# Moving a Fourier mixer into the attention steps of a two-block transformer kernel, with a half-spectrum transform

## The reference, cut to what matters

```
h = x
mod = silu(c) @ w_mod[0] + b_mod[0]          # sh1, sc1, g1, sh2, sc2, g2
u = modulate(rms_norm(x, norm1_g), sh1, sc1)
f, q, k, v = split(u @ w_in_even)            # f: 512 wide, 4 groups of 128
y_four = Re(FFT over tokens and the 128 features of a group of f)  @ w_four[group]
y_att  = window_attention(q, k, v, context keys and values, rpb)
h = h + g1 * (concat(y_four, y_att) @ w_out_even)
...
```

## Time and profile before

| what | value |
|---|---|
| median of 3 runs | 1970.37 us (1966.52 to 1971.26) |
| the profiled execution | 1971.28 us, of which the span is 1969.5 us |
| PE busy | 1932.1 us, 98% |
| DVE, ACT, POOL busy | 967.1, 685.3, 944.7 us |
| mean granted TensorE clock | 0.993 |

### The profile page before, as it was taken

One profiled execution on the slowest core, in us unless ns is written; L12 is line 12 of the kernel. 1 busy time (PEld: TensorE's weight loads), 2 busy tenths in 40 slices (PEclk: granted clock), 3 DMA queues, 4 the chain that ended last, 5 costly groups with the idle time before them and its releaser, 6 DMA issues. The chain is left out here.

```text
span 1969.5 us, 25202 instructions
## 1 busy us (share of the span) xinstructions
PE 1932.1 (98%) x9932; PEld 1587.5 (81%) x9932; DVE 967.1 (49%) x1515; ACT 685.3 (35%) x907; POOL 944.7 (48%) x699
## 2 busy tenths in 40 slices
PE   7998999999999999999999999999999999999998
PEld 6875787888888888888888667888888888888886
DVE  4666849783755762232333562467654462222132
ACT  4232733121223432221233554456554342122222
POOL 3334365665656454545474213434444464545454
PEclk9999999999999999999999999999999999999999
DMA  8553133744542322222313012221212222232211
GB/s 328 189 171 136 44 150 130 276 171 149 192 153 82 147 86 99 93 107 85 107 64 135 24 42 102 86 85 66 86 65 86 107 86 107 86 107 86 107 64 43
DMA packets 42786, 223.11 MB, mean 113 GB/s; under 512 B 12737, under 2 KB 13249, under 8 KB 17345
## 3 DMA queue, kind: packets, MB, share of 16 engines
q1 hardware_dynamic: 42688, 221.77, 30.8%
HBM read 217.55 MB, written 2.10 MB: 112 GB/s over the span
## 5 line engine op out<-in xcount | busy, mean ns | idle before, releaser
L1011 POOL TENSOR_TENSOR wl<-raw,wh 128x512 fp32r<-128x512 f32 x611 | 862.3, 1442 | 955.1 <-ACT wh L557 842.1
L1116 PE MATMUL bank<-uh,wh 128*128 128x512 f32 x1416 | 564.6, 399 | 2.6 <-POOL wl L1011 2.2
L1118 PE MATMUL bank<-uh,wl 128*128 128x512 f32 x1416 | 552.7, 390 | 0.0
L1117 PE MATMUL bank<-ul,wh 128*128 128x512 f32 x1416 | 552.5, 390 | 0.0
L557 ACT ACTIVATE wh<-raw 128x2048 fp32r<-128x2048 f32 (+1 forms) x148 | 279.4, 1888 | 571.4 <-PE bank L1118 562.3
L1116 PE MATMUL bank<-ah,wh 128*128 128x512 f32 x848 | 331.2, 391 | 1.1 <-DVE al L1973 1.1
L1117 PE MATMUL bank<-al,wh 128*128 128x512 f32 x848 | 330.4, 390 | 0.0
L1118 PE MATMUL bank<-ah,wl 128*128 128x512 f32 x848 | 330.2, 389 | 0.0
L1116 PEld LDWEIGHTS bank<-uh,wh 128*128 128x128 f32 x1416 | 266.1, 188 | 69.0 <-issue 10.2
L1117 PEld LDWEIGHTS bank<-ul,wh 128*128 128x128 f32 x1416 | 266.3, 188 | 56.5 <-issue 3.6
L1118 PEld LDWEIGHTS bank<-uh,wl 128*128 128x128 f32 x1416 | 266.2, 188 | 56.2
(11 more groups left out here) (285 smaller groups left out, 2117.5 us busy)
## 6 DMA issues: line engine op xcount, KB each, us to landing
raw<-in_w SPq DMA_DIRECT2D x64, 1024.0 KB, 4.8
mraw<-in_w_modr SPq DMA_DIRECT2D x36, 1024.0 KB, 4.8
raw<-in_w_gu SPq DMA_DIRECT2D x22, 1024.0 KB, 4.8
raw<-in_w_hg SPq DMA_DIRECT2D x16, 1024.0 KB, 4.8
raw<-in_w_in SPq DMA_DIRECT2D x8, 1024.0 KB, 9.5
modf<-in_w_modf SPq DMA_DIRECT2D x8, 1024.0 KB, 20.5
raw<-in_w_out SPq DMA_DIRECT2D x8, 1024.0 KB, 5.0
raw<-in_w_dn SPq DMA_DIRECT2D x8, 1024.0 KB, 4.8
```

Source lines behind the costliest of these rows:

```text
L1011: pool.tensor_tensor(wl[:, slot, c + k:c + k + 2], raw[:, b % RAW, k:k + 2], f32(wh[:, slot, c + k:c + k + 2]), ALU.subtract).then_inc(spl ...
L1116: pe.matmul(out, ah_, bh, start=first, stop=False)
L1117: pe.matmul(out, ah_, bl, start=False, stop=False)
L1118: return pe.matmul(out, al_, bh, start=False, stop=last)
```

## The change

1. **Fourier as filler.** The Fourier stage in front of the attention goes. `fourier_step(i)` is appended to attention step i: `fourier_y(g)` in steps 1, 5, 9, 13, the two parts of `fourier_out(g)` in the two steps behind it. All of it lies in PSUM bank 1, so scores go over three banks (4, 5, 0), and `scores(i)` waits for the first row maximum of pair i - 1 (before: both of pair i - 2). ACT gets `y_copy`, `sine_copy` and `four_high` between its copies and exponentials, DVE gets `four_out`, POOL gets `four_low`, two of the four folds and block 8's low part. The table products run half in block 7, half in step 0.
2. **Half spectrum.** The token transform computes frequencies 0 to 256 of the cosine part (three products of 257 columns) and 1 to 255 of the sine part (two of 255); `four_out` adds them for the lower frequencies and subtracts them, read backwards, for the upper ones.
3. **Modulation sums.** Sums 6 and 7 are cut in halves and lie in attention steps 2, 3, 6 and 7 on DVE; sums 8 to 11 stand behind the attention (before: 6 to 9 in the Fourier stage, 10 and 11 behind the attention). Loads 9 to 11 of `raw` are issued at the attention's end, since their places hold tables until then.
4. **Bias tables.** POOL makes 12 pairs of tables and not 16 (windows 1 and 2 share one).
5. **Start.** x is loaded ahead of `vecs` and `b_mod`, and the first weight block behind the first `modf`. PE no longer waits for `vecs` and `b_mod`. The sum of the squares is made on PE, chunk by chunk (`rows`), and not by seven DVE additions; an extra Sqrt early on ACT loads its table; the norm factor is a 128x128 reciprocal (`xrow`); `first_columns(0)` stands ahead of `norm_spread`, ACT's `split(0)` behind `rows_out(0)`, and there are `keep_clock` calls (1, 3 and 6 products) in between.

```diff
-COLUMNS = ("x", "ctx", "pool")
+COLUMNS = ("ctx", "pool")
-MOD_EARLY, MOD_MID = 6, 10
+MOD_EARLY, MOD_MID = 6, 8
+DFT_SIN, DFT_COS, DFT_END = 257, (512, 769), 1281
-        S_BANKS = [(4, 5), (0, 1)]
+        S_BANKS = (4, 5, 0)
+        def s_bank(i, e):
+            return bank[S_BANKS[(2 * i + e) % 3]]
+        DOT_STEP = {2: (6, 0), 3: (6, 1), 6: (7, 0), 7: (7, 1)}
+        Y_STEP = {1: 0, 5: 1, 9: 2, 13: 3}
...
 # SP
-            load(9, t["w_out"][1])
             for m in range(MOD_EARLY, MOD_MID):
                 load_mod(m)
-            sp.wait_ge(y_full, FG)
-            sp.dma_start(mask[:], t["mask"]).then_inc(tab_in, 16)
-            for b in range(10, 12):
-                load(b, t["w_out"][b - 8])
             sp.wait_ge(smax, 2 * len(PAIRS))
-            for m in range(MOD_MID, MOD0 + 2):
-                load_mod(m)
+            load_mod(8)
+            load_mod(9)
+            sp.wait_ge(four_full, FG)
+            load(9, t["w_out"][1])
+            sp.wait_ge(four_lo, FG)
+            load(10, t["w_out"][2])
+            load(11, t["w_out"][3])
+            load_mod(10)
+            load_mod(11)
+            load_mod(12)
+            load_mod(13)
...
 # ACT
             for i in range(len(PAIRS) + 2):
+                if i - 3 in Y_STEP:
+                    sine_copy(Y_STEP[i - 3])
+                if i - 4 in Y_STEP:
+                    four_high(Y_STEP[i - 4])
                 if i >= 2:
                     copy_pt(i - 2)
+                if i in Y_STEP:
+                    y_copy(Y_STEP[i])
                 if i < len(PAIRS):
                     exp(i)
...
 # PE
-            def fourier_out(g):
-                for a in range(4):
-                    last = pe.matmul(bank[4 + g % 2][:], ysb[:, g % 2, a, :], (dftc if a < 2 else dfts)[:, a % 2, :], start=(a == 0), stop=(a == 3))
-                last.then_inc(four_full, 1)
+            def fourier_out(g, part):
+                y, cosine = ysb[:, g % 2], bank[1][:, 0:DFT_SIN]
+                if part == 0:
+                    pe.matmul(cosine, y[:, 2, :], dft[:, 0:DFT_SIN], start=True, stop=False)
+                    pe.matmul(cosine, y[:, 0, :], dft[:, DFT_COS[0]:DFT_COS[0] + DFT_SIN], start=False, stop=False)
+                else:
+                    pe.matmul(cosine, y[:, 1, :], dft[:, DFT_COS[1]:DFT_COS[1] + DFT_SIN], start=False, stop=True)
+                    pe.matmul(bank[1][:, DFT_SIN:S], y[:, 2, :], dft[:, DFT_SIN:S], start=True, stop=False)
+                    pe.matmul(bank[1][:, DFT_SIN:S], y[:, 3, :], dft[:, DFT_COS[1] + DFT_SIN:DFT_END], start=False, stop=True).then_inc(four_full, 1)
+            def fourier_step(i):
+                if i == 0:
+                    channel_tables(1)
+                if i in Y_STEP:
+                    fourier_y(Y_STEP[i])
+                for part in range(2):
+                    if i - 1 - part in Y_STEP:
+                        fourier_out(Y_STEP[i - 1 - part], part)
...
             def scores(i):
                 if i == 0:
-                    pe.wait_ge(four_lo, 4)
...
                 else:
-                    pe.wait_ge(smax, 2 * (i - 1))
+                    pe.wait_ge(smax, 2 * i - 1)
...
                     turn(i - 2)
+                fourier_step(i)
...
 # DVE
+            def four_out(g):
+                cosine = bank[1][:, 0:DFT_SIN]
+                dve.tensor_tensor(four[:, 1:256], cosine[:, 1:256], sine[:], ALU.add)
+                dve.tensor_tensor(four[:, 257:512], bank[1][:, 255:0:-1], sine[:, ::-1], ALU.subtract)
+                dve.tensor_copy(four[:, 0:257:256], cosine[:, 0:257:256]).then_inc(four_ready, 1)
...
                     normalise(i - 1)
+                if i - 3 in Y_STEP:
+                    four_out(Y_STEP[i - 3])
+                if i in DOT_STEP:
+                    m, half = DOT_STEP[i]
+                    mod_dot(m, halves=(half,))
...
-            mod_dot(MOD_MID)
-            mod_dot(MOD_MID + 1)
+            for m in range(MOD_MID, MOD0):
+                mod_dot(m)
```

More of the change, by code:

```diff
@@ L621, in _ @@
             rows_out(0)
+            split(0)
             for k in range(KC):
@@ L682, in y_copy, with sine_copy, four_high @@
                     act.wait_ge(four_full, g - 1)
-                act.activation(ysb[:, g % 2], bank[6 + g % 2][:].rearrange("p (a n) -> p a n", a=4), ACT.Copy).then_inc(y_ready, 1)
-            y_copy(0)
-            for g in range(FG):
-                if g < FG - 1:
-                    y_copy(g + 1)
-                act.wait_ge(four_full, g + 1)
-                act.activation(uh[:, g, :], bank[4 + g % 2][:], ACT.Copy).then_inc(four_hi, 1)
+                act.activation(ysb[:, g % 2], bank[1][:].rearrange("p (a n) -> p a n", a=4), ACT.Copy).then_inc(y_ready, 1)
+            def sine_copy(g):
+                act.wait_ge(four_full, g + 1)
+                if g:
+                    act.wait_ge(four_ready, g)
+                act.activation(sine[:], bank[1][:, DFT_SIN:S], ACT.Copy).then_inc(sine_ready, 1)
+            def four_high(g):
+                act.wait_ge(four_ready, g + 1)
+                act.activation(uh[:, g, :], four[:], ACT.Copy).then_inc(four_hi, 1)
             def exp(i):
@@ L1054, in _, with four_low @@
+            def four_low(g):
+                pool.wait_ge(four_hi, g + 1)
+                pool.tensor_tensor(ul[:, g, :], four[:], f32(uh[:, g, :]), ALU.subtract).then_inc(four_lo, 1)
+            for b in range(2, 8):
+                split(b)
+            pool.wait_ge(split_lo, lows(7))
+            pool.memset(ff[:, :, 1, 0:1], 0.0)
+            fold(0)
+            pool.wait_ge(ctx_full, 4)
+            mod_summed(pool, MOD_EARLY - 1)
             pool.memset(tm[:, 0], 0.0).then_inc(tm_zero, 1)
-            pool.wait_ge(tm_zero, 1)
+            pool.memset(tm[:, 1], 0.0).then_inc(tm_zero, 1)
@@ L1068, in _ @@
+            bias_table(1)
+            fold(1)
+            split(8)
+            for t in range(2, 3 * len(PAIRS) // 4):
+                bias_table(t)
+                if t in (4, 7):
+                    fold(2 + (t - 4) // 3)
+                if t in (5, 8, 11):
+                    four_low((t - 5) // 3)
+            four_low(3)
             for b in range(8, 12):
@@ L1243, in silu_rows @@
                         last.then_inc(crow_full, 1)
-            pe.wait_ge(const_in, 48)
+            pe.wait_ge(const_in, 16)
             pe.wait_ge(csil_ready, 1)
             def sum_x():
-                pe.wait_ge(x_added, KC - 1)
-                for a in range(S // P):
-                    last = pe.matmul(bank[6][:, a:a + 1], sqx[:, KC - 1, P * a:P * a + P], ones_v[:, 0:1], start=(a == 0), stop=(a == S // P - 1), skip_group_check=True)
+                for k in range(KC):
+                    pe.wait_ge(sq_ready, k + 1)
+                    last = rows(bank[6], sqx[:, k], k == 0, k == KC - 1)
+                    if k % 2 == 0:
+                        keep_clock(1)
                 last.then_inc(sum_full, 1)
@@ L1304, in _ @@
             first_rows(0)
+            keep_clock(3)
+            first_columns(0)
             norm_spread("x")
-            first_columns(0)
+            keep_clock(6)
             first_rows(1)
@@ L1330, in _, with channel_tables @@
             pe.wait_ge(ulo_ready, 16)
+            def channel_tables(i):
+                pe.wait_ge(cw_ready, i) if i else pe.wait_ge(w4_in, 32)
+                if i == 0:
+                    pe.wait_ge(bank_free[bank_of(6, 1)], used(6) + 1)
+                for g in (2 * i, 2 * i + 1):
+                    for a in range(2):
+                        last = pe.matmul(bank[1][:, 2 * P * (g % 2) + P * a:2 * P * (g % 2) + P * a + P], cs[:, P * a:P * a + P], w4[:, g, :], start=True, stop=True)
+                last.then_inc(cw_full, 1)
             def beside(b):
                 def after(half):
+                    if (b, half) == (7, 0):
+                        channel_tables(0)
                     if (b, half) in HN_AFTER:
@@ L1434, in values @@
                     pe.wait_ge(vwin_in, 16 * 32)
+                    for half in range(2):
+                        pe.wait_ge(bank_free[bank_of(7, half)], used(7) + 1)
                 if w == 0 and hp >= 2:
```

214 lines of the change are left out of this document (97 added, 117 removed).

## The result

The changed kernel takes 1952.46 us in the median of four runs (1951.23 to 1952.93), the kernel before 1968.54 beside it (1966.52 to 1971.26). The ratio is 0.9923 with a 95% interval of 0.9911 to 0.9935, so the kernel is 13 to 18 us faster.

What follows compares the result with a forecast made beforehand. PE, busy 98% of the span, was taken as the bound. Terms -3.7 - 27.99 + 16.3 - 1.0 + 1.3 + 0.5 = -14.6 against 1971.28 gave 1956.7, stated as 1956.5 us, range 1950 to 1963.

Steps and rivals of the forecast that it cites:

- The first scaling: Sign at the start: DVE's first scaling of a chunk would stand at 17 to 18 us and not at 21.07.
- L1508 waits for `pT`: Sign of being wrong: in the attention, the values products (L1508) would wait for the copies `pT`.
- Start, -3.7: Start of the kernel: earlier x and a shorter chain bring the first scaling 3 to 4 us earlier, taken as 3.7.
- The bounds 0 to 5: Limits given for the start's saving: 0 if transfers hold the rest, 5 if extra `keep_clock` products keep chunks at 2.4 GHz.
- Fourier stage and filler, -27.99 + 16.3: Ahead of the attention: the 27.99 us stage goes; table, `fourier_y` and `fourier_out` products add 16.3 to PE, net -11.7.
- Filler in gaps, -1.0: Attention steps 0 to 2: some filler lies where PE waits for DVE and ACT while the pipeline fills, -1.0 us.
- New waits in the steps, +1.3: Attention steps 7 and 8: half sums delay the row maximum and scores wait 0.5 to 0.8 us twice, +1.3.
- Behind the attention, +0.5: After the attention: four sums are just hidden under two blocks, bank 0 back at B + 20 to 21.7, +0.5 us.
- DVE through POOL: Rival in the attention steps: sums always meet POOL's tables or folds and DVE becomes the bound, +4.5, 1961 us; chance 0.12.
- Start lost to transfers: Rival at the start: `modf` chunks arrive late and the ladder ends as before, 1960.4 us; chance 0.07.
- Four sums not hidden: Rival behind the attention: one load 5 us late makes PE wait 5 us before block 10, 1961.5 us; chance 0.05.
- ACT's insertions: Rival in the attention: 12 inserted ACT copies hold the pipeline; no change (1971 us) chance 0.06, slower (+25, 1982) chance 0.08.

Runs made afterwards that it cites:

- `before_again`: The kernel before, unaltered, run again for a second profile: 1969.14 us (one run).
- `more_behind`: The changed kernel with four more DVE operations, each of half a sum's size, behind the fourth sum after the attention: 1959.28 us, ratio 0.9957.
- `short_start`: The changed kernel with 8 and not 16 `keep_clock` products ahead of the row sums and none between them: 1949.57 us, ratio 0.991.
- `both`: The changed kernel with the fewer `keep_clock` products of `short_start` and with sums 6 to 9 inside the attention: 1949.28 us, ratio 0.991.
- `start_only`: The kernel before with only the new start: 1966.50 us against 1967.73, ratio 0.9994.
- `after_again`: The changed kernel, unaltered, timed and profiled once more: 1952.12 us, ratio 0.9922.
- `full_columns`: The changed kernel computing 2,048 columns a Fourier group and not 1,281, by copies of products that are then overwritten: 1956.33 us, ratio 0.9943.
- `tables_early`: The changed kernel with POOL's bias tables no longer waiting for the scalings of that step: 1954.18 us, ratio 0.9934.

## Why the prediction was right, step by step

The forecast was 1956.5 with a sum of -14.6; the medians differ by 16.1 and, in the second rounds, 15.1. The mechanism was right: PE's list decides, and the attention part brought nearly all of it. That the sum came so close is luck, since two errors of size nearly cancelled, 2 us too much at the start and 2.9 too little in the attention. The time itself is 4.0 below the forecast, mostly because the sum was taken from one execution of 1971.28, and the median of the kernel before beside the changed one was 1968.54.

The range of 1950 to 1963 held it, but its lower end was not what its terms give. A start gain of 5 (1.3 more) and no new waits (1.3 less) make 1953.9 and not 1951, and 1952.46 lies below that; at the other end, a start gain of 1.5 and twice the waits make 1960 and not 1961.

Two signs went otherwise than said. The first scaling came at 18.66 and not at 17 to 18. And L1508 waits for `pT`, one of the signs of being wrong, twice 0.8 in the last steps; these are waits that the kernel before had three times, so the sign was drawn too wide.

**Start, -3.7.** Mis-sized: 1 to 2 us. The steps were right as far as they went (x earlier, additions and table load gone from the chain, reciprocal 0.95), but the root came at 15.54 and not 14.5, since PE's own `keep_clock` products, taken for harmless, paced the row sums. The saving was also read against one execution with a late x and a low clock; the second one ended block 7 2.2 us earlier. For the spread's 2.08 us the prediction named the clock of 20 to 30 us, but the spread stood at 18.10 to 20.18, and there, from 18 to 20 us, the clock was 0.50: with x and clock as in `before_again` it takes 1.16. The bounds 0 to 5 held the term. The page "ScalarE: Activation LUTs" of the Trainium skill (What ACT_TABLE_LOAD costs) would have made this term larger by 1.4, to -5.1; no trace here comes near it, the largest difference of two being 4.2 (164.63 less 160.42), between the slowest old and the fastest new start.

**Fourier stage and filler, -27.99 + 16.3.** The filler came to 1.95 for the tables and 3.49 a group, 15.9 in all: 0.4 less than said. The 3.49 is the group's 16.01 less four steps of 3.13.

**Filler in gaps, -1.0.** It was -2.2. Steps 0 to 3 grew from 8.98 (201.60 - 192.62) to 12.17 us, 3.19, although they got 3.49 of filler and the 1.06 us of tables not in block 7: 1.36 fell into gaps. The tail from step 15 to block 8 grew from 10.84 to 11.27, 0.43, with 1.29 of filler: another 0.86, which the prediction did not count. One wait of 0.8 for `pT` went with it.

**New waits in the steps, +1.3.** None. The hand-worked steps had the scalings at their mean of 707 ns, which holds the meetings with POOL; but since the tables wait for `p_norm`, 11 of the 16 pairs take 0.88 or 0.89, and 32 scalings in the steps average 568 ns. DVE is busy 14.0 of 16.0 us in the fullest group, for the 15.7 of the prediction, and PE waits for no row maximum. The three errors make 0.4 + 1.2 + 1.3 = 2.9, the whole of -14.3 against -11.4.

**Behind the attention, +0.5.** No PE wait in front of block 10, so 0, and its account held to a microsecond: addition at B + 19.2, bank given back by B + 20.6, needed at B + 21.8. `more_behind` shows the price beyond it: more than the prediction's 1 us for each us of lateness, since the clock fell too.

**Rivals.** DVE through POOL: five of the 16 pairs of scalings still take 1.06 to 1.75 us, but PE waits for none; worth 1 to 2 us if the rest were let in. Start lost to transfers: true in part at most. 1 to 2 of 3.7 are left, but PE waits for `modf` only 0.2 us in the changed kernel, so the rest is put down to PE's own list and to the first trace, as above; the transfers show once the start is short (`short_start`, `both`). Four sums not hidden: no. ACT's insertions: no, with at least as much room again.

## What to carry to other kernels

When PE is busy 98% of the span, cost a change as PE's own list: products that vanish, products that are added, and the gaps that added products fill; here that gave 14.3 us in the three traces of either attention, to 0.05. Count in the waits of the stage that goes, and what they cost the clock behind them. The start, where the transfers are saturated, differed by 2 us from one execution of the kernel before to the next, so profile such a stretch twice before a saving is read from it. And look at what shares an engine in order (a semaphore that keeps POOL off DVE's scalings, a split that waits ahead of another's part): one such line was worth about as much as the whole new start, 1 to 2 us.

## What was unexpected of the hardware

- PE's granted clock took its lower level (1.2 GHz) in different places in executions of one program: 0.81 and then 1.00 from 20 to 30 us in the two traces of the kernel before. It fell behind stretches in which PE had idle time, but not each time: `short_start` was busy 7.52 us of the ten ahead and got 0.83, `both` had 7.73 and got 1.00. In the old Fourier stage it fell each time, behind the wait of 2.25 us or so for POOL's fold: 0.54, 0.58 and 0.50 over 3 us in the first trace, `before_again` and `start_only`. That part of the loss went with the stage.
- Between the span and the time of the run lay 1.7 to 1.9 us in every execution of the kernel before and of `start_only`, but 2.0 to 4.1 in the four of the changed kernel, 2.1 to 3.2 in those of `after_again`, and as little as 1.8 in others with the new attention (`full_columns`, `tables_early`). So a part of what a span gains may not show in the time; why is open.
- When DVE and POOL meet, either can be the one that is held up. In the changed kernel a half sum begins at 173.91 and a pair of tables on POOL at 174.14: the sum keeps its 1.22, and the pair takes 2.26 where it takes 1.42 otherwise, as these rows of POOL's timeline show.

```profile
174.14 2.26 POOL L1097 TENSOR_TENSOR tm<-tab,mask 128x256 f32<-128x256 f32 x2 [1.09 <-DVE sc L1966]
...
178.71 1.42 POOL L1097 TENSOR_TENSOR tm<-tab,mask 128x256 f32<-128x256 f32 x2 [0.82 <-DVE sc L1966]
```
